# GpSimd's order in a mixing cell: mask of the attention exponentials and low part of a weight chunk change places

## What is computed

```
causal = key_pos < q_pos
log_1m = where(causal, -softplus(z), 0)
after  = cumsum(log_1m, reverse) - log_1m
w      = where(causal, exp(log_sigmoid(z) + after), 0)
o      = w @ v
```

## Time and profile before

| | |
|---|---|
| median of 3 runs | 4707.87 us |
| the profiled execution's own time | 4709.19 us |
| its span (first to last instruction) | 4707.4 us |
| mean granted TensorE clock | 0.984 of full speed |
| TensorE matmul busy | 4533.5 us, 96% of the span |
| VectorE busy | 2797.4 us, 59% |
| ScalarE busy | 1691.5 us, 36% |
| GpSimd busy | 1720.9 us, 37% |

### The profile page before, as it was taken

The page is one execution under the profiler, slowest core; times in us unless marked ns, Lnnn a source line. Parts: engine busy times, 40 slices in busy tenths (PEclk is TensorE's granted clock), DMA queues, the critical chain, the costliest instruction groups (busy, mean ns, idle before and its releaser), DMA issues. The chain is left out here.

```text
span 4707.4 us, 62035 instructions
## 1 busy us (share of the span) xinstructions
PE 4533.5 (96%) x21780; PEld 3650.0 (78%) x21780; DVE 2797.4 (59%) x4484; ACT 1691.5 (36%) x2701; POOL 1720.9 (37%) x1058
## 2 busy tenths in 40 slices
PE   7999999989999989999999999999999999999998
PEld 5777767757787768888888878887888888888886
DVE  5776777785351377777777657774444444444444
ACT  3555556565242343333333434443111111111121
POOL 2444344431211247777777731111222222222221
PEclk9999999989999999999999999999999999999999
DMA  2111111124331222222222335557644444444441
GB/s 82 45 50 50 46 50 49 42 77 174 130 120 42 104 75 98 97 98 96 90 97 97 109 101 211 211 215 282 196 143 151 139 146 145 152 137 146 147 138 63
DMA packets 260434, 546.15 MB, mean 116 GB/s; under 512 B 17152, under 2 KB 148480, under 8 KB 247808
## 3 DMA queue, kind: packets, MB, share of 16 engines
q1 hardware_dynamic: 255616, 476.41, 30.4%
q10 hardware_dynamic: 4608, 67.11, 3.4%
HBM read 375.16 MB, written 168.30 MB: 115 GB/s over the span
## 5 line engine op out<-in xcount | busy, mean ns | idle before, releaser
L155 PE MATMUL spread_g<-spread_ahi,spread_vhi 128*128 128x512 f32 x2048 | 799.2, 390 | 7.9 <-DVE spread_alo L2645 4.5
L156 PE MATMUL spread_g<-spread_alo,spread_vhi 128*128 128x512 f32 x2048 | 798.1, 390 | 0.0
L157 PE MATMUL spread_g<-spread_ahi,spread_vlo 128*128 128x512 f32 x2048 | 798.1, 390 | 0.0
L2711 DVE TENSOR_TENSOR spread_acc<-spread_acc,spread_g 128x512 f32<-128x512 f32 x492 | 338.0, 687 | 704.9 <-PE spread_g L157 704.9
L2645 POOL TENSOR_TENSOR spread_vlo<-spread_vraw,spread_vhi 128x1024 fp32r<-128x1024 f32 x128 | 324.7, 2537 | 1051.1 <-ACT spread_vhi L2844 1036.1
L155 PE MATMUL shared_carry<-shared_wide_hi,shared_w_hi 128*128 128x512 f32 x1408 | 559.7, 397 | 28.8 <-DVE shared_wide_lo L583 11.2
L156 PE MATMUL shared_carry<-shared_wide_lo,shared_w_hi 128*128 128x512 f32 x1408 | 554.6, 394 | 0.0
L157 PE MATMUL shared_carry<-shared_wide_hi,shared_w_lo 128*128 128x512 f32 x1408 | 554.0, 393 | 0.0
L188 POOL TENSOR_TENSOR shared_w_lo<-shared_w_raw,shared_w_hi 128x1024 fp32r<-128x1024 f32 x94 | 242.9, 2585 | 618.7 <-ACT shared_w_hi L184 568.5
L155 PEld LDWEIGHTS spread_g<-spread_ahi,spread_vhi 128*128 128x128 f32 x2048 | 385.2, 188 | 89.7 <-issue 5.5
L156 PEld LDWEIGHTS spread_g<-spread_alo,spread_vhi 128*128 128x128 f32 x2048 | 385.4, 188 | 80.3 <-issue 0.2
(11 more groups left out here) (308 smaller groups left out, 9017.2 us busy)
## 6 DMA issues: line engine op xcount, KB each, us to landing
gates<-spread_stage ACTq DMA_DIRECT2D x32, 2048.0 KB, 16.8
spread_act<-gelu_u SPq DMA_DIRECT2D x128, 512.0 KB, 3.4
spread_vraw<-in_peer_v SPq DMA_DIRECT2D x128, 512.0 KB, 6.5
spread_graw<-gates SPq DMA_DIRECT2D x128, 512.0 KB, 4.5
shared_raw<-in_select_pairs SPq DMA_DIRECT2D x54, 1024.0 KB, 5.1
gelu_u<-front SPq DMA_DIRECT2D x184, 256.0 KB, 2.0
shared_w_raw<-in_w_mix SPq DMA_DIRECT2D x56, 512.0 KB, 3.7
join_uraw<-in_peer_u SPq DMA_DIRECT2D x36, 512.0 KB, 4.4
```

What stands on the lines that cost most here:

```text
L155: nc.tensor.matmul(out, whi, xhi, start=(first and i == 0), stop=False)
L156: nc.tensor.matmul(out, whi, xlo, start=False, stop=False)
L157: mm = nc.tensor.matmul(out, wlo, xhi, start=False, stop=(last and i == len(terms) - 1))
L2711: nc.vector.tensor_tensor(acc[:, k, h * H:h * H + H], before[:, h * H:h * H + H], ops[:, d, h], ALU.add).then_inc(added, 1)
```

## The change

In each masked cell GpSimd now masks the two heads' exponentials first and makes the weight chunk's low part after that. Nothing else is touched: the instructions, their sizes, their waits and the other engines' orders are the same.

```
                     low_part(pool, nc.gpsimd, j, 0, i)
+                    if masked[i]:
+                        for s in range(2):
+                            mask(s, wt_raw, wt, wt_done, j, i)
                     for g in ends[i - 1] if i else ():
                         c, h = GROUPS[g]
                         if c != "turn" and h == 1 and c + 2 < more:
                             n, _, slot = chunk(*following(j, par, jj), c + 2)
                             w.split_low(pool, n, slot)
-                    if masked[i]:
-                        for s in range(2):
-                            mask(s, wt_raw, wt, wt_done, j, i)
```

## The result

| | before | after |
|---|---|---|
| median of 5 runs | 4707.94 us | 4729.54 us (4727.66 to 4732.85) |
| ratio | | 1.0047, 95% interval 1.0037 to 1.0058 |
| the profiled execution's own time | 4709.19 us | 4727.66 us |
| its span | 4707.4 us | 4725.8 us |
| GpSimd busy | 1720.9 us | 1711.7 us |

The kernel became 21.6 us slower, 0.46%. The time lies in the stated range; the forecast of 14.5 us was short by 7 us, or a third of the loss. In the profiles the last product of pair 6 stands at 979.73 before and at 1003.81 after, 24.1 us later; from there to the end the profiled execution of after was 5.7 us shorter (24.1 less the 18.4 between the spans). The change moves nothing in that part, and over the eleven profiles of this study it takes between 3722.0 and 3731.0 us, so I take the 5.7 us for variation and not for an effect of the change.

A forecast was written before the change was run, and what follows sets the result against it. TensorE was taken to bound pairs 0 to 6. A late sum in cell 3 (10.5 us) and a wait for chunk 4 (4.0) made 14.5 us on 4707.9, so 4722.4 us; range 4711 to 4736, forecast's own 4718 to 4730.

The forecast's parts named there:

- What bounds the kernel: Pairs 0 to 6: TensorE, busy 833.0 of 865 us, works through its list almost without a break.
- Term 1: Cell 2 into cell 3: low part holds up VectorE's two taps, TensorE's sum 1.52 us late; 7 x 1.5 = 10.5 us.
- Term 2: Cell 5: TensorE waits for chunk 4's low part, 0.63 us in six pairs, 0.18 in pair 6; 4.0 us.
- At nothing: Chunks 2, 3, 5, 6, later softplus masks, cells 4, 7, 8 and weight loads: delays covered, no cost.
- The clock: TensorE's granted clock in cell 3: the forecast counted no falls despite the new idling.
- the falls in several pairs: Rival, cell 3: clock falls cost 1.7 us each; in every pair 26.4 us in all, 4734; chance 0.15.
- A granted clock at 0.50 in cell 3: Sign that the forecast is wrong: TensorE's clock at its 1.2 GHz level instead of 2.4 there.
- only chunk 4: Rival: no collision in cell 2 or more room into cell 3; only 4.0 us lost, 4712; chance 0.12.
- no effect: Rival: TensorE's waits fall into idling it already has, or all shifts alike; 4708; chance 0.07.
- faster: Rival: cell 3's taps and masks, no longer held up by the low part, gain 10.6 us; 4697; chance 0.04.
- the taps of cell 3: Gain claimed in pairs 1, 3, 5: the low part no longer blocks a VectorE tap, 2.2 us each.
- the earlier masks: Gain claimed in cell 3 of pairs 0, 2, 4, 6: masks no longer held back, 1.0 us each.

The follow-up runs named there:

- the fourth run: Masks put ahead of the low part in cells 3, 6 and 7 only, against the kernel before: 4706.25 us, ratio 0.9997.
- the second run: Masks put ahead of the low part in cell 2 only, against the kernel before: 4728.26 us, ratio 1.0043.

## Why the prediction was right, and where it fell short

*What bounds the kernel.* Right: every delay of TensorE in pairs 0 to 6 stayed; none was won back by the end of pair 6.

*Term 1, 10.5 us.* It measured 11.4. The mechanism is the one forecast, step by step: taps of 4.65 us, softplus 2.08 late (2.06 forecast), the sum 1.63 late (1.52). The missing 0.1 is the start behind a wait, which the sum of rows had at nothing: TensorE's sum starts 0.15 us after the low part's end (157.01 to 157.16). In pair 6 too the low part won, though the tap is recorded as issued 0.01 us ahead of it:

```profile
908.61 4.81 DVE L634 SCALAR_TENSOR_TENSOR front<-mix_u,mix_cwj,front 128x1024 f32<-128x1024 f32 x2 [0.17 <-DVE mix_u L605]
...
908.62 2.39 POOL L188 TENSOR_TENSOR shared_w_lo<-shared_w_raw,shared_w_hi 128x1024 fp32r<-128x1024 f32 x1
```

*Term 2, 4.0 us.* It measured 5.1, again short by the start behind a wait (0.16 of 0.79 us). That the low part would run unhindered in 2.4 us was right.

*At nothing.* Right for cells 3, 6 and 7, by the fourth run. No wait for a weight load shows on TensorE's list.

*The clock.* This is the step that failed. The forecast had the clock at nothing; the falls in several pairs stood as a rival with 0.15, 1.7 us each, on the ground that the earlier trace rows kept its clock with idling of about a microsecond. It was the wrong row to compare: that place idled 0.8 us, and with the change it idles 1.75 in the same few microseconds. What came was the forecast's two terms, 16.5 us, and the rival's falls in four pairs of seven, 1.4 to 2.7 us each and 7.3 together in the trace, where the forecast had none and the rival 11.9 for all seven. "A granted clock at 0.50 in cell 3" was one of the prediction's own signs of being wrong, and it came. 4729.54 lies 0.5 us inside the forecast's own range (4718 to 4730) and also in the rival's (4726 to 4738); that it lies in the range stated for the whole, 4711 to 4736, is owed to a range that took in most of this rival. The two terms alone, had both been sized right, give 4724.4.

The other rivals are out: "only chunk 4" by the second run, "no effect" and "faster" by the result; the taps of cell 3 and the earlier masks gained nothing, since TensorE had the 4 us to spare that were read. The taps didn't even become faster: with the low part moved behind the masks it meets the two taps at the end of cell 3 instead (4.78 us for two, as in the fourth run).

## What to carry to other kernels

GpSimd work that reads SBUF can be free at one place of a cell and dear 5 us later, with every wait and duration unchanged, if a VectorE instruction with two SBUF inputs stands at the new place: look at VectorE's timeline there and at what waits behind it. Ask of moved cover first whether it hid in a wait that nobody else needed; here it did, and the masks put ahead of it were wanted by nobody for another 4 us or more. When a change adds idling to TensorE, add up all idling within the same few microseconds, what was there before included, and count the clock as a term if the sum is above what kept its clock elsewhere (here 0.8 and 1.0 us kept it, 1.55 to 1.9 lost it in some pairs).

## What the runs showed that was not expected

A wait of TensorE for its own matmuls, 0.30 and 0.48 us of idle time in the rows, cost 1.27 us in cell 3, and next to nothing in cell 11, where another wait took its place. And the clock's falls are not tied to a pair: with the same delay in all seven pairs they came in pairs 0, 3, 4 and 5 in one kernel and in 0, 1, 2 and 3 in another. What decides in which pairs it falls was not tried further; each kernel has one profile, so how the falls vary from run to run stays open, as do the 5.7 us by which the stages behind pair 6 were shorter in the profile of after.
